# One softmax over three dilated groups, run between the quarters of its own projection

## The chip, the cores and the metric

The kernel runs on one core of a Trainium2 chip, in float32 from input to output. The metric is the device time of one execution, in microseconds (us). Engines: TensorE (PE in the profile, its weight loads PEld), VectorE (DVE), ScalarE (ACT), GpSimd (POOL) and SyncE (SP), which issues most DMAs.

## The reference, cut to what matters

512 positions of 1024 features go through two layers. Each layer is a mixer, a layer norm, a mixture of experts (top 2 of 32), and a layer norm. The change is in the second layer's mixer:

```
def odd_mixer(x, w_in, w_out):
    p = (x @ w_in).reshape(B, T, 3, 3, DIL_HEADS, DIL_DH)      # group, q/k/v, 8 heads of 64
    slopes = alibi_slopes(DIL_HEADS)
    for g, (window, dilation) in enumerate(((128,1), (512,4), (2048,16))):
        o, l = dilated_band_attention(p[:, :, g, 0], p[:, :, g, 1], p[:, :, g, 2],
                                      window, dilation, slopes)
        outs.append(o); lses.append(l)
    wts = jax.nn.softmax(jnp.stack(lses, 0), axis=0)
    y = jnp.einsum('gbth,gbthd->bthd', wts, jnp.stack(outs, 0))
    return y.reshape(B, T, DIL_W).astype(x.dtype) @ w_out
```

A query t of a group sees the keys t, t-d, t-2d, ... within the window, with scores q.k/8 minus slope times distance. Each group has its own softmax, and the three outputs are weighted by the softmax of their log-sum-exps. With 512 positions that is the same as one softmax over all keys of the three groups together.

## The kernel before, in words

x stands turned in `xt_hi` and `xt_lo`, the high and the low part of its numbers; each weight chunk is split likewise by ScalarE (`split_unit`, L676, the high part) and VectorE (L952, the rest), so that a product is three matmuls: hi x hi, hi x lo, lo x hi. A *unit* is half the contraction of 512 output features: four quarters of 12 matmuls of 128x512 each. The input projection of the second layer has 18 units (`chunk`, `unit`, matmuls on L1542), its results go to two alternating sets of four PSUM banks, and are copied out four at a time (`evacuate`, L682 and L960). SP loads a unit's weights (1 MB) when the split of the unit two before it has been done.

After the last unit attention begins. It goes over four pairs of heads, and for each pair over two heads and two layers of work (near: group 0, with 256 keys for each tile of 128 queries; far: groups 1 and 2, whose queries and keys are sorted by residue modulo 4, so that a tile holds one residue): 16 steps of four tiles. The queries of the other head of the pair are zero in `qz`, so that the contraction is 128. A step is: `odd_scores` (L1903 to L1910), `biased` (L1439, adds slope times distance and takes the maximum), `exps` (L906), `weights_t` (L1921, transposes), `keep_weights` (L916, L1450, PSUM to SBUF), `odd_mix` (L1935 to L1940), `keep_out` (L1457). Scores run one step ahead. Far and near have softmaxes of their own; the far rows are written to DRAM and read back in order of position, and the two are merged there by maxima and denominators (L1479 to L1500). Then y is turned (L1959), split in two parts and multiplied with the output weights (`out_and_logits`, L1648). Tile by tile VectorE adds the residual and takes the norm's statistics (`out_norm`, L1203 to L1212), ScalarE normalises, TensorE turns the rows (L1658) and computes the router's logits (L1666). The router's index arithmetic and the experts follow; SP loads the weights of the experts in three buffers, which overlap the tiles of the mixer, with `load_pair`.

Every engine has its list of instructions in program order; the order around the change is written out by hand, and semaphores tie the engines together.

## Time and profile before

| | us |
|---|---|
| median of 3 runs | 1295.38 (1289.61 to 1295.59) |
| the profiled execution | 1293.89, its span 1292.1 |
| TensorE matmul busy | 1050.3 (81%) |
| VectorE, ScalarE, POOL busy | 499.9, 296.4, 134.7 |
| mean granted TensorE clock | 0.916 of full speed |

Busy times of TensorE count overlapping matmuls once. Its matmuls are pipelined: a 128x512 matmul lasts 0.39 us and the next starts 0.23 us after it. The order of stages in time: first layer's mixer to about 285 us, its router and experts to 600, second layer's norm and projection to 820, attention and merge to 948, output projection, router, experts and the last norm.

### The profile page before, as it was taken

What the parts mean: (1) busy time and instruction counts of PE and PEld (TensorE: products, weight loads), DVE (VectorE), ACT (ScalarE), POOL (GpSimd) and SP (SyncE); (2) the same over time, 40 slices, a digit from 0 to 9 for tenths busy, and PEclk for the clock granted to TensorE, in tenths of its full rate; (3) what the DMA queues carried; (4) which work ended last, traced back from release to release, by engine and by line L of the source; (5) the groups of instructions that cost most, each with busy time, mean ns of one, the idle gap of its engine ahead of it and who ended that gap; (6) DMA issues with size and microseconds to landing.
All of it is one profiled execution on the core that took longest, in us unless ns stands there. A gap on an engine that the chain in (4) does not pass through costs nothing.

```text
span 1292.1 us, 14037 instructions
## 1 busy us (share of the span) xinstructions
PE 1050.3 (81%) x5044; PEld 717.8 (56%) x5044; DVE 499.9 (39%) x1201; ACT 296.4 (23%) x567; POOL 134.7 (10%) x191
## 2 busy tenths in 40 slices
PE   6999999998798788850999999688477788787850
PEld 5878888886343233320788889578466333233320
DVE  3853675555333111118422222454265333111118
ACT  3343312221112111110321212243211121111110
POOL 5000000000121111110000000121010111111110
PEclk8989999996899999995899999898677899999995
DMA  8244331449699999934233223000159699999943
GB/s 219 66 72 92 69 95 66 160 182 385 228 421 423 424 425 424 424 160 182 98 98 97 97 98 98 1 9 16 43 208 381 248 422 425 424 424 424 424 161 167
DMA packets 68845, 286.87 MB, mean 222 GB/s; under 512 B 12268, under 2 KB 14332, under 8 KB 43184
## 3 DMA queue, kind: packets, MB, share of 16 engines
q1 hardware_dynamic: 52992, 234.96, 48.2%
q10 hardware_dynamic: 5184, 33.56, 6.2%
q0 software_dynamic: 10608, 17.54, 3.7%
q8 instruction: 37, 0.61, 0.2%
q14 instruction: 24, 0.20, 0.0%
HBM read 281.79 MB, written 24.15 MB: 237 GB/s over the span
## 4 chain that ended last, share of the span: by engine, by line
PE 59%; DMA 14%; SPq 11%; DVE 9%; issue 5%; ACT 2%; ACTq 0%; POOLq 0%; DVEq 0%; POOL 0%
PE bank L1542 15%; PE bank L1621 14%; DMA wgu<-in_w_up 10%; PE bank L1822 8%; SPq L392 6%; SPq L397 4%; PE bank L1844 4%; PE bank L1648 4%; PE bank L1639 2%; DVE h L1380 2%; PE bank L1910 1%; PE bank L1723 1%; PE bank L1708 1%; PE bank L1811 1%; PE bank L1666 1%
## 5 line engine op out<-in xcount | busy, mean ns | idle before, releaser
L1822 PE MATMUL bank<-wgu,xgt 128*64 128x512 f32 x1024 | 234.3, 610 | 31.3 <-DMA wgu<-in_w_up 27.9
L1822 PEld LDWEIGHTS bank<-wgu,xgt 128*64 128x64 f32 x1024 | 86.1, 141 | 175.1 <-issue 159.3
L1844 PE MATMUL bank<-wd,htt 128*64 128x512 f32 x512 | 116.9, 597 | 49.9 <-issue 48.5
L952 DVE TENSOR_TENSOR wl<-raw,wh 128x2048 fp32r<-128x2048 f32 x40 | 91.6, 2290 | 146.4 <-ACT wh L676 146.4
L676 ACT ACTIVATE wh<-raw 128x2048 fp32r<-128x2048 f32 x40 | 76.6, 1915 | 192.5 <-PE bank L1621 104.8
L1346 DVE TENSOR_TENSOR hh<-sg,bank 128x256 f32<-128x256 f32 x32 | 13.5, 421 | 233.2 <-ACT sg L837 233.2
L1844 PEld LDWEIGHTS bank<-wd,htt 128*64 128x64 f32 x512 | 40.4, 136 | 104.3 <-issue 104.3
L1542 PE MATMUL bank<-xt_hi,wh 128*128 128x512 f32 x192 | 75.4, 393 | 2.7 <-DVE wl L952 2.7
L1542 PE MATMUL bank<-xt_hi,wl 128*128 128x512 f32 x192 | 75.2, 392 | 0.0
L1542 PE MATMUL bank<-xt_lo,wh 128*128 128x512 f32 x192 | 75.2, 392 | 0.0
L1351 DVE COPY yt<-bank 128x512 f32<-128x512 f32 x32 | 22.1, 692 | 135.1 <-PE bank L1844 135.1
L829 ACT ACTIVATE xgt<-bank,lnt 128x128 f32<-128x128 f32 x136 | 51.2, 456 | 70.3 <-PE bank L1811 70.3
L837 ACT ACTIVATE sg<-bank 128x256 f32<-128x256 f32 x32 | 12.3, 385 | 223.9 <-PE bank L1822 223.9
L1621 PE MATMUL bank<-xt_hi,wh 128*128 128x512 f32 x128 | 52.6, 411 | 7.4 <-DVE wl L952 7.4
L1338 DVE TENSOR_SCALAR xgt<-bank,lnt 128x128 f32<-128x128 f32 x136 | 46.4, 403 | 16.9 <-PE bank L1811 16.8
L1621 PE MATMUL bank<-xt_hi,wl 128*128 128x512 f32 x128 | 51.5, 402 | 0.0
L1621 PE MATMUL bank<-xt_lo,wh 128*128 128x512 f32 x128 | 51.3, 401 | 0.0
L1621 PE MATMUL bank<-wh,xt_hi 128*128 128x512 f32 x128 | 50.6, 395 | 0.0
L847 ACT ACTIVATE yt<-bank 128x512 f32<-128x512 f32 x32 | 19.1, 597 | 136.5 <-PE bank L1844 120.0
L1621 PE MATMUL bank<-wh,xt_lo 128*128 128x512 f32 x128 | 49.9, 390 | 0.0
L574 POOL DMA_INDIRECT y_rows<-yt,td x20 | 24.4, 1219 | 244.8 <-ACT yt L847 164.3
L1621 PE MATMUL bank<-wl,xt_hi 128*128 128x512 f32 x128 | 49.9, 389 | 0.0
(333 smaller groups left out, 1759.5 us busy)
## 6 DMA issues: line engine op xcount, KB each, us to landing
wgu<-in_w_gate SPq DMA_DIRECT2D x64, 1024.0 KB, 22.7
wgu<-in_w_up SPq DMA_DIRECT2D x64, 1024.0 KB, 25.7
wd<-in_w_down SPq DMA_DIRECT2D x36, 1024.0 KB, 25.4
wd<-in_w_down ACTq DMA_DIRECT2D x28, 1024.0 KB, 12.4
raw<-in_w_in_odd SPq DMA_DIRECT2D x18, 1024.0 KB, 4.9
raw<-in_w_in_even SPq DMA_DIRECT2D x16, 1024.0 KB, 7.3
y<-y_rows SPq DMA_DIRECT2D x8, 1024.0 KB, 8.5
h<-in_x SPq DMA_DIRECT2D x8, 512.0 KB, 5.1
```

The lines of the kernel that those rows point to most:

```text
L392: sp.dma_start(wgu[s][:, b, i, :, :].rearrange("p k f -> p (k f)"), w[l][ds(e, 1)].rearrange("a (p k) f -> p (a k f)", p=P)).then_inc(wgu_ ...
L397: sp.dma_start(wd[s][:, b, :, :].rearrange("p k n -> p (k n)"), w_down[l][ds(e, 1)].rearrange("a (p k) n -> p (a k n)", p=P)).then_inc(wd_ ...
L676: act.activation(wh[slot][:, :, :], raw[slot][:, :, :], ACT.Copy).then_inc(w_hi, 1)
L829: ins = act.activation(xgt[:, k, :], bank[0][:, k * P:(k + 1) * P], ACT.Identity, scale=lnt[:, l, 0, k:k + 1], bias=lnt[:, l, 1, k:k + 1])
L952: dve.tensor_tensor(wl[slot][:, :, :], raw[slot][:, :, :], wh[slot][:, :, :], ALU.subtract)\
L1338: ins = dve.tensor_scalar(xgt[:, k, :], bank[1][:, (k - 4) * P:(k - 3) * P], lnt[:, l, 0, k:k + 1], lnt[:, l, 1, k:k + 1], ALU.mult, ALU.add)
L1380: link(dve.scalar_tensor_tensor(h[:, t, :], y2[t][:, c * D:(c + 1) * D], ga[:, c, t:t + 1], h[:, t, :], ALU.mult, ALU.add))
L1542: ins = pe.matmul(out_of(i), a, b, start=(k == 0 and n == 0), stop=(k == nk - 1 and n == 2))
L1621: ins = pe.matmul(bank[i][:, :], a, b, start=(k == 0 and n == 0), stop=(k == 7 and n == 2))
L1648: ins = pe.matmul(bank[4 * c + t][:, :], yp[:, kk, t * P:(t + 1) * P], wp[c][:, kk, :], start=(first and kk == 0 and n == 0), stop=(kk == ...
L1822: ins = pe.matmul(bank[2][B * b:B * (b + 1), :], xgt[:, k, B * b:B * (b + 1)], wgu[s][:, b, :, k, :], start=(k == 0), stop=(k == KT - 1))
L1844: ins = pe.matmul(bank[5 + n][B * b:B * (b + 1), :], htt[:, k, B * b:B * (b + 1)], wd[s][:, b, k, n * 512:(n + 1) * 512], start=(k == 0), ...
```

## The change

All eight heads get one softmax over the 512 columns that a tile of 128 queries has: 256 near keys, 128 of group 1 and 128 of group 2. The step is now one tile of a pair of heads (`n` from 0 to 15: pair `n // 4`, tile `n % 4`), both heads at once, each in its own half of the array's rows (64 features), with no zero padding. In each tile the queries stand by residue modulo 4 (32 of each), so that a far product is 32 queries of one residue by the 128 keys of that residue, written to 32 of the bank's partitions. Slopes move into the queries' scale and the exponential's scale, so that one table of distances serves all heads. The weights are turned by a product with a diagonal that holds 1 over the denominator. The mix gives the heads' outputs already turned (64 features by 512 positions, two heads one above the other), so that the merge, the far rows in DRAM and the turning of y are gone.

The projection goes in another order: q and k of the first four heads of the three groups, then v for the far groups and for group 0, then q and k of the other four heads and the rest of v. All its chunks use banks 0 to 3, emptied tile by tile (`keep_odd`), and banks 4 to 7 hold the scores. Attention's steps stand between quarters of units 6 to 17 (`q(m, i)`), by an order written out for each engine. The output projection starts with the first features while the last pair is being done. SP loads the first experts' gate and up weights before the output projection; one pair of experts, not two, is loaded behind it.

```diff
+        ODD = ((0, 0), (1, 0), (2, 0), (None, 0), (None, None), (0, 1), (1, 1), (2, 1), (None, 1))
@@ SyncE
+            for m in range(18):
+                (g, o), u = ODD[m // 2], U_ODD + m
+                sp.wait_ge(w_lo, u + 1)
+                w = xo[m % 2 * 4 * P:(m % 2 + 1) * 4 * P, :]
+                if o is None:
+                    src = w[:, 2 * C:3 * C].rearrange("(k p) c -> p k c", p=P)
+                    sp.dma_start(raw[m % 2][:, :, :], src).then_inc(raw_in[m % 2], 16)
+                    continue
+                src = w.rearrange("(k p) (g s o c) -> p k g s o c", p=P, g=3, s=3, o=2)
                 for i in range(2):
-                    for half in range(2):
-                        load_unit(4 * g + (U_ODD + 2 * i + half), half, xo, half * 4 * P,
-                                  ds(g * (3 * C) + i * C, C))
-            for g in range(3):
-                for half in range(2):
-                    load_unit(U_ODDV + 2 * g + half, half, xo, half * 4 * P,
-                              slice(3 * C * g + 2 * C, 3 * C * (g + 1)))
+                    part = src[:, :, i + 1, 2, o, :] if g is None else src[:, :, g, i, o, :]
+                    sp.dma_start(raw[m % 2][:, :, 256 * i:256 * (i + 1)], part).then_inc(raw_in[m % 2], 16)
...
+            sp.wait_ge(unit_done, U_WOUT2 + 2)
+            load_gate_up(1, 0, (0, 1))
+            sp.wait_ge(w_lo, U_WOUT2 + 2 + 2)
+            load_down(1, 0, (0, 1))
+            sp.wait_ge(yl, 4)
             load_pair(1, 2, (4, 5))
             sp.wait_ge(unit_done, U_WOUT2 + 2 + 2)
-            load_pair(1, 0, (0, 1))
             load_pair(1, 1, (2, 3))
...
@@ POOL
+            for t in (2, 3):
+                wait_ln(pool, 1, t)
+            pool.iota(near0[:, :], pattern=[[1, 256]], base=-P, channel_multiplier=-4, **exact)
+            for i in range(2):
+                pool.iota(near1[:, i, :], pattern=[[4, 224]], base=-4 * 96, channel_multiplier=-4, **exact)
+            pool.iota(jdiff[:, :], pattern=[[-1, 224]], base=224, channel_multiplier=1).then_inc(near_ready, 1)
...
@@ ScalarE
+            def keep_odd(c, i):
+                if i < 3:
+                    act.wait_ge(bank_done, 3 * (8 + c) + i + 1)
+                else:
+                    act.wait_ge(unit_done, U_ODD + 2 * c + 4)
+                g, o = ODD[c]
+                if o is None:
+                    ins = act.activation(v3[:, 0, i, :], bank[i][:, :], ACT.Copy)
+                elif g is None:
+                    ins = act.activation(v3[:, 1:3, i, 256 * o:256 * (o + 1)],
+                                         bank[i][:, :].rearrange("p (g c) -> p g c", g=2), ACT.Copy)
+                elif g == 0:
+                    ins = act.activation(kg0[:, 2 * o + i - 2, :], bank[i][:, :], ACT.Copy)
+                else:
+                    ins = act.activation(k12[:, 2 * o + i - 2, g - 1, :].rearrange("p (a j) -> p a j", a=4),
+                                         perm(bank[i][:, :]), ACT.Copy)
+                ins.then_inc(kept[i], 1)
+            def exps(n):
+                hp, t = divmod(n, NT)
+                act.wait_ge(nm_ready, n + 1)
+                for b in range(2):
+                    s = sc[n % 2][b][:, (0 if t else P):T]
+                    ins = act.activation(s, s, ACT.Exp, scale=SLOPES[2 * hp + b], bias=nm[:, n, b:b + 1],
+                                         accum_out=dn[:, n, b:b + 1])
...
+            def keep_weights(n):
...
+                act.activation(pts[hp // 3][0][:, T * t + lo:T * (t + 1)], bank[4 + 2 * (n % 2)][:, lo:T], ACT.Copy)\
+                   .then_inc(pta, 1)
+            def heads_hi(hp):
+                act.wait_ge(o2_ready, hp + 1)
+                act.activation(in_row_order(yo_hi[:, hp, :]), in_step_order(bank[3 if hp == 2 else 6][:, :]), ACT.Copy).then_inc(yh, 1)
...
+            for m in range(16):
+                if m:
+                    split_unit(U_ODD + m + 1, (m + 1) % 2)
+                if 6 <= m < 14:
+                    exps(m - 6)
+                if m in (10, 14):
+                    heads_hi((m - 10) // 4)
+                if m % 2:
+                    keep_odd(m // 2, 2)
+                if 6 <= m < 14:
+                    keep_weights(m - 6)
+                if m % 2:
+                    keep_odd(m // 2, 3)
+            split_unit(U_ODD + 17, 1)
+            exps(8)
+            exps(9)
+            keep_weights(8)
+            exps(10)
+            keep_weights(9)
+            exps(11)
+            keep_weights(10)
+            split_unit(U_WOUT2, 0)
+            exps(12)
+            keep_weights(11)
+            exps(13)
+            keep_weights(12)
+            exps(14)
+            keep_weights(13)
+            keep_odd(8, 2)
+            keep_odd(8, 3)
+            exps(15)
+            keep_weights(14)
+            heads_hi(2)
+            split_unit(U_WOUT2 + 1, 1)
+            keep_weights(15)
+            heads_hi(3)
...
@@ VectorE
+            def q_scales():
+                for i in range(8):
...
+                dve.wait_ge(near_ready, 1)
+                far_ = near_t[:, :].rearrange("p (g c) -> p g c", g=2)
...
+            def biased(n):
...
+                for b in range(2):
+                    s, d = bank[4 + 2 * (n % 2) + b], sc[n % 2][b]
+                    dve.tensor_tensor_reduce(out=d[:, lo:256], in0=s[:, lo:256], in1=near0[:, lo:256],
+                                             scale=1.0, scalar=-3.0e38, op0=ALU.add, op1=ALU.max,
+                                             accum_out=mm[:, n, b, 0:1])
+                    ins = dve.tensor_tensor_reduce(out=d[:, 256:T].rearrange("p (g c) -> p g c", g=2),
+                                                   in0=s[:, 256:T].rearrange("p (g c) -> p g c", g=2),
+                                                   in1=near1[:, :, 96 - 32 * t:224 - 32 * t],
                                                    scale=1.0, scalar=-3.0e38, op0=ALU.add, op1=ALU.max,
-                                                   accum_out=mm[lay][:, t:t + 1])
+                                                   accum_out=mm[:, n, b, 1:2])
+            def diagonals(n):
+                dve.wait_ge(p_ready, n + 1)
+                link(dve.reciprocal(rd[:, n, :], dn[:, n, :]))
+                for b in range(2):
+                    ins = dve.tensor_scalar(dg[n % 2][b][:, :], ident[:, :], rd[:, n, b:b + 1], None, ALU.mult)
+                ins.then_inc(dg_ready, 1)
...
+            def heads_lo(hp):
+                dve.wait_ge(yh, hp + 1)
+                dve.tensor_tensor(in_row_order(yo_lo[:, hp, :]), in_step_order(bank[3 if hp == 2 else 6][:, :]),
+                                  in_row_order(yo_hi[:, hp, :]), ALU.subtract).then_inc(yl, 1)
+            for m in range(16):
+                if m:
+                    split_unit(U_ODD + m + 1, (m + 1) % 2)
+                if m == 1:
+                    q_scales()
+                if m == 2:
+                    distances()
+                if m % 2:
+                    keep_odd(m // 2, 0)
+                if 6 <= m < 14:
+                    biased(m - 6)
+                if m % 2:
+                    keep_odd(m // 2, 1)
+                if 6 <= m < 14:
+                    diagonals(m - 6)
+                if m in (10, 14):
+                    heads_lo((m - 10) // 4)
+                if 6 <= m < 14:
+                    keep_weights(m - 6)
...
+            biased(12)
+            keep_weights(11)
+            diagonals(12)
+            keep_odd(8, 0)
+            biased(13)
+            keep_weights(12)
+            diagonals(13)
+            keep_odd(8, 1)
+            biased(14)
+            keep_weights(13)
+            diagonals(14)
+            biased(15)
+            keep_weights(14)
+            diagonals(15)
+            heads_lo(2)
+            split_unit(U_WOUT2 + 1, 1)
+            keep_weights(15)
+            heads_lo(3)
...
@@ TensorE
+            def odd_part(v, tiles):
+                c, half, slot = v // 2, v % 2, v % 2
+                g, o = ODD[c]
...
+                for i in tiles:
+                    if half == 0 and c:
+                        pe.wait_ge(kept[i], 8 + c)
+                    for kk in range(4):
+                        k = 4 * half + kk
+                        for n, (xp, wp) in enumerate(((xt_hi, wh), (xt_hi, wl), (xt_lo, wh))):
+                            if o is None:
+                                a, b = in_order(xp, k, i), wp[slot][:, kk, :]
+                            elif g is None:
+                                a, b = by_residue(xp, k, i), wp[slot][:, kk, :]
+                            else:
+                                a, b = wp[slot][:, kk, i * P:(i + 1) * P], xp[:, k, :]
+                            ins = pe.matmul(bank[i][:, :], a, b, start=(k == 0 and n == 0), stop=(k == 7 and n == 2))
+                    if half and i < 3:
+                        ins.then_inc(bank_done, 1)
+                if tiles[-1] == 3:
+                    ins.then_inc(unit_done, 1)
+            def odd_scores(n):
+                hp, t = divmod(n, NT)
+                st = 4 + 2 * (n % 2)
+                if t == 0:
+                    for i in (hp % 2, 2 + hp % 2):
+                        pe.wait_ge(kept[i], 8 + (8 if hp > 1 else 3))
+                if n >= 2:
+                    pe.wait_ge(pta, n - 1)
+                    pe.wait_ge(ptd, n - 1)
...
+                rows_of = [slice(64 * b, 64 * (b + 1)) for b in range(2)]
+                for b, r in enumerate(rows_of):
+                    lo = 0 if t else P
+                    pe.matmul(bank[st + b][:, lo:256], qg0[r, hp, t * P:(t + 1) * P],
+                              kg0[r, hp, (t - 1) * P + lo:(t + 1) * P], start=True, stop=True)
+                for g in range(2):
+                    for a in range(4):
+                        for b, r in enumerate(rows_of):
+                            ins = pe.matmul(bank[st + b][32 * a:32 * (a + 1), 256 + g * P:256 + (g + 1) * P],
+                                            q12[r, hp, g, t * P + 32 * a:t * P + 32 * (a + 1)],
+                                            k12[r, hp, g, a * P:(a + 1) * P], start=True, stop=True)
...
+            def weights_t(n):
+                t, st = n % NT, 4 + 2 * (n % 2)
+                pe.wait_ge(dg_ready, n + 1)
+                for k in range(0 if t else 1, 4):
+                    for b in range(2):
+                        ins = pe.matmul(bank[st + b][:, k * P:(k + 1) * P], sc[n % 2][b][:, k * P:(k + 1) * P],
+                                        dg[n % 2][b][:, :], start=True, stop=True)
...
+            def odd_mix(hp):
...
+                out_of = [bank[3 if hp == 2 else 6][64 * b:64 * (b + 1), :] for b in range(2)]
+                cols = [slice((2 * hp + b) * DH, (2 * hp + b + 1) * DH) for b in range(2)]
+                for s in (0, 2, 1, 3):
+                    w = 1 if s == 3 else 2
+                    for b in range(2):
+                        at = T * s + P
+                        src = pts[hp // 3][b][:, at:at + P] if s == 3 else \
+                            pts[hp // 3][b][:, at:at + 2 * 384].rearrange("p (u c) -> p u c", u=2)[:, :, 0:P]
+                        pe.matmul(out_of[b][:, s * P:(s + w) * P], v3[:, 0, s, cols[b]], src,
+                                  start=(s == 0), stop=False)
+                for g in range(2):
+                    for a in range(4):
+                        for b in range(2):
+                            at = 256 + g * P + 32 * a
+                            ins = pe.matmul(out_of[b].rearrange("p (t c) -> p t c", t=NT)[:, :, 32 * a:32 * (a + 1)],
+                                            v3[:, 1 + g, a, cols[b]],
+                                            pts[hp // 3][b][:, :].rearrange("p (t c) -> p t c", t=NT)[:, :, at:at + 32],
+                                            start=False, stop=(g == 1 and a == 3))
...
+            def odd_out(t, c, kks):
+                for kk in kks:
+                    for n, (yp, wp) in enumerate(((yo_hi, wh), (yo_hi, wl), (yo_lo, wh))):
+                        ins = pe.matmul(bank[4 * c + t][:, :], yp[:, kk, t * P:(t + 1) * P], wp[c][:, kk, :],
+                                        start=(kk == 0 and n == 0), stop=(kk == 3 and n == 2))
+                return ins
+            for m in range(16):
+                n = m - 6
+                q(m, 0)
+                if 0 <= n < 8:
+                    odd_scores(n)
+                q(m, 1)
+                if m in (10, 14):
+                    odd_mix((m - 10) // 4)
+                q(m, 2)
+                if 0 <= n < 8:
+                    weights_t(n)
+                q(m, 3)
+            q(16, 0)
+            odd_scores(8)
+            q(16, 1)
+            odd_scores(9)
+            weights_t(8)
...
+            odd_scores(14)
+            weights_t(13)
+            q(17, 3)
+            odd_scores(15)
+            weights_t(14)
+            odd_mix(2)
+            def first_features(t):
+                pe.wait_ge(kept[t], 17)
+                odd_out(t, 0, range(2))
+            pe.wait_ge(w_lo, U_WOUT2 + 3)
+            first_features(0)
+            first_features(1)
+            weights_t(15)
+            first_features(2)
+            odd_mix(3)
+            pe.wait_ge(yl, 3)
+            first_features(3)
+            pe.wait_ge(w_lo, U_WOUT2 + 4)
+            odd_out(0, 1, range(3))
+            odd_out(0, 0, (2,))
+            pe.wait_ge(yl, 4)
+            for t in range(NT):
+                odd_out(t, 1, range(0 if t else 3, 4))
+                last = odd_out(t, 0, range(2 if t else 3, 4))
+                if t < 3:
+                    last.then_inc(tile_out, 1)
+                else:
+                    last.then_inc(unit_done, 2)
+            normed_logits(1)
```

## Rows read from the trace of the kernel before

**Rows 1.** The page: TensorE's busy share, the granted clock in 40 slices.

```profile
PE 1050.3 (81%) x5044; PEld 717.8 (56%) x5044; DVE 499.9 (39%) x1201; ACT 296.4 (23%) x567; POOL 134.7 (10%) x191
...
PEclk8989999996899999995899999898677899999995
```

**Rows 2.** Chain of waits, second mixer: start, length, work (xcount: instructions).

```profile
620.75 199.10 PE bank L1542 x864
...
851.54 0.88 PE bank L1921 x8
852.42 1.79 PE bank L1910 x16
...
947.62 23.81 PE bank L1648 x96
```

**Rows 3.** Stretches: length; busy PE, PEld, DVE, ACT, POOL; clock; DMA.

```profile
819.90:830.20 10.30, 0.00 (x0) 0.00 (x0) 7.84 (x6) 4.14 (x4) 0.00 (x0) 0.75 0.00 0
830.20:923.60 93.40, 78.74 (x552) 74.07 (x552) 43.60 (x191) 39.33 (x144) 18.59 (x15) 0.88 0.03 9
923.60:942.50 18.90, 0.11 (x2) 0.00 (x0) 8.71 (x16) 0.46 (x2) 5.79 (x4) 0.51 0.27 73
942.50:947.60 5.10, 3.68 (x16) 3.28 (x16) 4.55 (x7) 3.13 (x5) 0.00 (x0) 0.50 0.43 146
```

**Rows 4.** Groups by shape, 818 to 935 us: busy us, mean ns, idle before.

```profile
L906 ACT ACTIVATE sc<-sc,nm 128x256 f32<-128x256 f32 x56 | 27.7, 495 | 30.9 <-DVE nm L1443 30.9
L1439 DVE CUSTOM_DVE_ANT_0 sc<-bank,bh 128x256 f32<-128x256 f32 x56 | 20.5, 420 | 8.0 <-PE bank L1910 7.3 <-issue 0.7
...
L906 ACT ACTIVATE sc<-sc,nm 128x128 f32<-128x128 f32 x8 | 3.2, 397 | 16.6 <-DVE nm L1443 16.6
```

**Rows 5.** Chain of waits: first projection, tiny matmuls; expert products, transposes behind.

```profile
48.78 16.33 PE bank L1621 x72
...
78.04 1.02 PE bank L1600 x32
...
1015.51 7.09 PE bank L1822 x32
...
1029.26 6.87 PE bank L1822 x32
1036.12 1.09 PE bank L1811 x8
```

**Rows 6.** Groups by shape of VectorE and ScalarE, 620 to 822 us.

```profile
L952 DVE TENSOR_TENSOR wl<-raw,wh 128x2048 fp32r<-128x2048 f32 x19 | 43.5, 2291 | 85.9 <-ACT wh L676 85.9
...
L959 DVE TENSOR_SCALAR q<-bank 128x512 f32 x4 | 2.6, 686 | 13.5 <-PE bank L1542 13.5
...
L676 ACT ACTIVATE wh<-raw 128x2048 fp32r<-128x2048 f32 x19 | 36.4, 1918 | 76.1 <-PE bank L1542 76.1
```

**Rows 7.** The page's DMA issues: count, KB each, us to landing.

```profile
raw<-in_w_in_odd SPq DMA_DIRECT2D x18, 1024.0 KB, 4.9
```

**Rows 8.** Timeline of SP: first expert weights behind the output projection.

```profile
971.46 0.33 SPq L392 DMA_DIRECT2D wgu<-in_w_gate  x1
```

**Rows 9.** DMA rate from 900 to 1040 us in 40 slices.

```profile
GB/s 7 68 5 0 0 0 0 84 166 143 0 2 19 360 426 424 424 150 0 180 176 338 394 425 427 421 438 421 433 419 335 276 25 67 0 222 428 419 406 423
```

**Rows 10.** Timeline of VectorE: the last output tile's statistics, first and last.

```profile
971.47 1.29 DVE L1203 SCALAR_TENSOR_TENSOR h<-h,bank 128x512 f32<-128x512 f32 x2 [0.28 <-PE bank L1648]
...
976.48 0.16 DVE L1212 SCALAR_TENSOR_TENSOR nmr<-mv,rstd 128x1 f32<-128x1 f32 x1
```

**Rows 11.** Stretches of the first layer, columns as in rows 3.

```profile
68.00:70.00 2.00, 2.00 (x4) 0.35 (x2) 1.93 (x3) 0.00 (x0) 0.00 (x0) 0.50 1.02 158
70.00:72.00 2.00, 2.00 (x6) 1.61 (x6) 1.48 (x3) 1.08 (x2) 0.44 (x1) 0.50 0.83 128
...
140.00:160.00 20.00, 20.00 (x99) 16.50 (x98) 16.27 (x51) 8.00 (x18) 2.79 (x1) 1.00 0.30 53
```

**Rows 12.** Timeline of TensorE, first layer: products with 4 rows.

```profile
65.05 5.01 PE L1586 MATMUL bank<-mrow,sel 4*128 4x512 f32 x8
```

More of the change, by code:

```diff
@@ L125, in trunk @@
         mask = const.take("mask", [P, P], f32)
-        near = const.take("near", [P, 2, 256], f32)
+        near0 = const.take("near0", [P, 256], f32)
         before = const.take("before", [P, P], bf16)
@@ L145, in trunk @@
         eq = lngb_z.take("eq", [P, 8, NCOL], f32)
+        lngb_z = Zone(const.at, 8 * KB)
+        sc = [[lngb_z.take(f"sc{i}{b}", [P, T], f32) for b in range(2)] for i in range(2)]
         lngb_z = Zone(const.at, 8 * KB)
@@ L1461, in pair_steps @@
-            def pair_steps(hp, last):
-                for k in range(4):
-                    if not (last and k == 3):
-                        biased(hp, k + 1)
-                    keep_weights(hp, k)
-                    if k:
-                        keep_out(hp, k - 1)
-                keep_out(hp, 3)
-            biased(0, 0)
-            with dve.Fori(0, 3) as hp, link.rolled(hp, 4, 3):
-                pair_steps(hp, False)
-            pair_steps(3, True)
-            dve.wait_ge(far_in, 32)
@@ new lines, in _ @@
+            split_unit(U_ODD + 17, 1)
+            biased(8)
+            diagonals(8)
+            biased(9)
+            keep_weights(8)
+            diagonals(9)
+            biased(10)
+            keep_weights(9)
+            diagonals(10)
+            biased(11)
+            keep_weights(10)
+            diagonals(11)
+            split_unit(U_WOUT2, 0)
+            biased(12)
[4 more added lines that the diff above has]
+            keep_weights(12)
@@ L1550, in by_residue @@
                 return perm(xp[:, k, :])[:, i, :]
-            def chunk(c, a, u, st, x_cols=None, xt_from=None):
-                pe.wait_ge(ev_d, c + 1)
-                if a is not None:
-                    pe.wait_ge(ev_a, a + 1)
-                for half in range(2):
-                    unit(u + half, half, half, lambda i: bank[st + i][:, :], x_cols, xt_from=xt_from)
             pe.wait_ge(ident_ready, 1)
```

442 lines of the change are left out of this document (121 added, 321 removed).

## The prediction

> **What bounds the kernel now.** I read the row of busy shares and the granted clock in forty slices first [rows 1]: TensorE is busy 81% of the span, and the stretch of slices 26 to 30 is where it is idle or slow. The chain of waits over the second layer's mixer then gives the stage [rows 2]. The projection is one piece of TensorE work, 199.10 us from 620.75, with nothing between its 864 matmuls. The output projection starts at 947.62 and takes 23.81 us, so it ends at 971.43. The 127.8 us between (947.62 - 819.85) are attention alone. The table of stretches splits them [rows 3]: 10.3 us with TensorE idle while the padded queries are staged; 93.4 us of head steps with TensorE busy 78.7 us at a mean clock of 0.88; 18.9 us in which it works 0.11 us (far rows to DRAM and back, merge); and 5.1 us of turning y at clock 0.50. The whole mixer, 620.75 to 971.43, takes 350.7 us. Behind it stand the router and then the experts, whose weights stream at 424 GB/s.
>
> So attention pays latencies in turn: scores, biasing, exponentials, weights turned, copied, mixed. The change puts these steps between quarter units of the projection. What counts then is TensorE's own work, if every latency fits behind it.
>
> **TensorE's work after the change.**
> - Projection: again 18 units of 48 matmuls, and again 192 of them read x by residue. 199.1 us stays.
> - Near scores: 32 products with a contraction of 64 rows, two heads on the two halves of the array. Full-array products of this type cost 1.79 us for 8 with 128 columns (16 instructions), 0.224 each [rows 2], so 0.448 for 256 columns. In turn: 24 x 0.448 + 8 x 0.224 = 12.5 us; side by side 6.3 (the first tile of each pair has 128 near keys).
> - Far scores: the tile's queries stand by residue, so each residue has a product of 32 queries by 128 keys: 16 per tile for two heads and two groups, 256 in all. At the full-array price 256 x 0.224 = 57.3 us. No row shows 64*32 pieces of the array. The nearest is the expert product in two 64-column halves: 16 products of 512 columns take 6.87 us, 0.429 each [rows 5], where 512 columns at 0.224 per 128 would be 0.896; two halves run as one. The lower bound is issue: 32 tiny matmuls take 1.02 us, 0.032 each [rows 5], and each product is two instructions, so 512 x 0.032 = 16.4 us. I take factor two, the nearest row: 28.7 us for far, 6.3 for near, 35.0 together; bounds 22.7 (6.3 + 16.4) and 69.8.
> - Weights turned: no longer transposes (0.88 us for 8) but products with a diagonal of 1/denominator, 1.79 us for 8 [rows 2]: (16 x 8 - 4 x 2) x 0.224 = 26.9 us, where transposes would cost 13.2. This edit costs time, and buys the whole merge.
> - Mixing: output 64 rows high, two heads in the two column halves, the case that [rows 5] shows. Near 24 x 0.448 + 8 x 0.224 = 12.5, far 64 x 0.224 = 14.3; halved, 13.4 us.
> - Output projection: 96 matmuls, now without a cold start. 72 in 16.33 us is 0.2268 each [rows 5]: 21.8 us.
> - Changes of the array's shape: three per tile and two per mix, 16 x 3 + 4 x 2 = 56. After the expert product in halves, 8 transposes take 1.09 us, in the attention loop the same 8 take 0.88 [rows 2, 5]: 0.21 for a return to the full shape, of which there are 20. The 36 others have no row; bounds nothing and 0.21, I take half. Together 4.2 + 3.8 = 8.0 us.
>
> Sum: 199.1 + 35.0 + 26.9 + 13.4 + 21.8 + 8.0 = 304.2 us against 350.7: 46.5 us less.
>
> The Trainium skill (TensorEngine Tiling, Key Properties) says that changing the tiling mode drains the engine, which speaks against this change; the 0.21 us agrees in kind, and without any such cost the forecast would be 8 us lower. The same skill (TensorE: Matmul & The Clock Gate, part 3) has 16 pieces of 32 by 32 run 10.6 times as fast; by it the far scores would fall to their lower bound, and the time would be that of the first rival below. No row here shows it or excludes it.
>
> **Does every latency fit?** One unit is 48 x 0.2268 = 10.9 us, a quarter 2.72. In units 6 to 13 a step is quarter, scores (2.2), quarter, quarter, weights, quarter. From the end of scores to the weights there are two quarters, 5.4 us. In that time VectorE does four reductions (56 in 20.5 us, 0.37 each [rows 4]: 1.5) and two small operations (0.3), ScalarE two exponentials of 512 (256 take 0.50, 128 take 0.40 [rows 4], so 0.69 each, and 0.2 for reading the sum: 1.6), VectorE the reciprocal and two diagonals (0.6, an estimate: three operations near the 0.2 us that its small ones take), handovers 0.4: 4.4 us. VectorE is free to start: the split of the next unit ends about 1.9 + 2.3 us after the unit begins, plus 0.7 for a kept bank [rows 6], near 5.0, when scores end too (2.72 + 2.2). Slack some 1 us. Of VectorE's 15 us step, at most 2.3 + 1.8 + 0.6 + 0.7 + 1.4 = 6.8 are used. All projection chunks now share four banks; each is emptied by 0.69 us three quarters before it is needed.
> In units 16 and 17 a tile's period is 2.72 + 2.2 + 1.8 + 0.45 = 7.2 us on TensorE; VectorE, in order, needs its 4.4 us loop per tile plus 2.3 twice for splits. It fits. Past the last quarter, the last tile's latency stands behind its scores, turned weights, mix 2 and two pieces of the output projection, about 8 us; mix 3 waits for a weight split and two copies, and here I see the two sides within 0.5 us. I allow 2 us for such waits over the whole mixer.
>
> **Moved or added, hidden.** SP's queue: the weights come in half loads with 1 KB runs, two issues a unit; a unit's load took 4.9 us in the page's DMA list [rows 7] and has the rest of one unit and a whole one, about 17 us, so it may double. Four stores to the far rows, two small ones and two loads go. The first pair of experts is now issued before the output projection and only one pair remains after it; before, the two pairs issued from 971.46 kept DMA near its full rate to about 1005, dropping to 25 GB/s by 1010, and the experts began at 1015.5 [rows 5, 8, 9], so this gains nothing and loses nothing. POOL stages nothing; its five tables are written right after the norm and read two units later. VectorE's sixteen memsets and thirteen distance operations (about 5 us) stand in units 1 and 2, which have over 5 us free each. In the first layer POOL and VectorE lose some set-up; there the chain is TensorE without a gap, so 0.
>
> **Late behind it.** Output tiles now end 12.2, 8.1, 4.1 and 0 us before the end (18 matmuls each) rather than in pairs. VectorE needs 5.2 us from a tile to its statistics [rows 10]. Tile 1 ends its at -2.9 (two rows of sums 2.9, scale 2.3), tile 2 at +2.3, tile 3 at +7.5 where it was +5.2 (971.47 to 976.64). The last normalised tile is turned at once if late; before it had 4.5 us to spare, but tile 2 delays the turning too. I charge 2.2 us.
>
> Gain 46.5 - 2 - 2.2 = 42.3 us. The profiled run took 1293.89 us (span 1292.1), 1.5 under the median of 1295.38, within the spread of the three runs. That gives 1251.6 on the profiled run and 1253 on the median: I forecast 1252.
>
> **Rivals.**
> 1. The small pieces run eight at a time. Scores cost 22.7, not 35.0: 12.3 less, 1240. For: independent halves already run fully beside each other [rows 5]. Against: two heads write different banks from the same columns, which no row shows. Then VectorE's 4.4 us loop is still under the 6.4 us period.
> 2. They run in turn. Scores cost 69.8: 34.8 more, 1287. For: only column halves are shown, never rows split. Against: the halves in [rows 5].
> 3. Slower than before, by the clock. Around 67 us TensorE was busy all the time with products of 4 rows and the clock still fell to 0.50 (68 to 72 us) [rows 11, 12]: being busy does not hold it. Score stretches of 2 us with 64 by 32 pieces recur for over 190 us. Each us of full-speed work done at 1.2 GHz costs one more, so from 42.3 us of such work on (a fifth of the interleaved stretch of some 200 us) the change loses; at a half of it, 100 us, it is 1252 + 100 = 1352. Against: in the first layer attention between projection quarters ran at 1.00 throughout (140 to 160 us) [rows 11], and here every gap is filled with full-array work.
> 4. It does not overlap as it says: some step's latency is over 5.4 us, and TensorE waits at each of 16 tiles. At 1.5 us each, 24 us: 1276. Against: the slack worked out.
>
> **Chances.** Forecast 0.52, rival 1 0.20, rival 2 0.11, rival 3 0.06, rival 4 0.11. Rivals 1, 2 and 4 all stay faster; of rival 2 and 4 together a little would come to no change. Under 0.5% (6.5 us, what the runs can tell) I put 0.05, slower 0.06, faster 0.89. Range 1235 to 1283: it holds rivals 1 and 4 and leaves out rival 3 and most of rival 2.
>
> **What would show it.** Near and far scores of a tile: 2.2 us if factor two, 1.4 if eight, 4.4 in turn. Projection matmuls 0.227 apart at clock 1.00 throughout. TensorE busy without gaps from 621 to about 927, and the output projection ending there instead of at 971. Everything behind it shifted and equally long. A mean clock under 0.9 in that stretch, or VectorE as releaser of the diagonal products in many tiles, would prove me wrong.

## Result, and the profile after

The changed kernel took 1232.08 us (median of 4 runs, 1228.44 to 1235.47) against 1294.35 for the kernel before: ratio 0.9514, interval 0.949 to 0.9537. The forecast was 1252 with a range of 1235 to 1283: the sign was right, the gain 20 us too small, and the time 3 us below the range. The profiled execution took 1234.14 us, 59.8 less than the 1293.89 before.

The page of the changed kernel, busy time of each engine, then TensorE and its granted clock in forty slices, answers to [rows 1]:

```profile
PE 1033.2 (84%) x5484; PEld 690.9 (56%) x5484; DVE 493.3 (40%) x1237; ACT 288.8 (23%) x501; POOL 107.4 (9%) x159
...
PE   6999999999688878875199999999996888787850
...
PEclk8989999998699999998599999999986999899985
```

Slices 21 to 30 hold the mixer: TensorE full and at full clock, where before slices 26 to 30 were partly idle or slow. The stretches below answer to [rows 3]; columns are busy us and instructions of PE, PEld, DVE, ACT and POOL, the granted clock, DMA share and GB/s.

```profile
620.50:690.10 69.60, 69.60 (x300) 57.85 (x300) 25.59 (x46) 16.34 (x14) 0.00 (x0) 0.98 0.33 106
690.10:832.30 142.20, 142.20 (x987) 118.95 (x986) 54.79 (x135) 43.13 (x63) 0.00 (x0) 1.00 0.23 75
832.30:883.00 50.70, 49.95 (x541) 43.06 (x541) 30.03 (x117) 20.18 (x44) 0.00 (x0) 1.00 0.24 89
883.00:907.10 24.10, 24.10 (x147) 19.93 (x146) 13.09 (x30) 4.87 (x6) 0.00 (x0) 1.00 0.95 367
907.10:955.50 48.40, 35.18 (x153) 25.98 (x151) 25.25 (x123) 8.23 (x16) 6.77 (x7) 0.68 0.57 218
955.50:1232.40 276.90, 196.42 (x928) 83.98 (x928) 76.44 (x143) 45.35 (x113) 35.82 (x45) 0.91 0.84 350
```

The whole mixer now takes 286.6 us (620.5 to 907.1) in place of 350.7, which is 64.1 less; from the output projection's end to the first expert product it is 48.4 in place of 44.1, 4.3 more; the experts take 276.9, before 276.6 (1292.1 - 1015.5). 64.1 - 4.3 = 59.8: that is the whole difference.

The chain of waits in the first interleaved steps (start, us, what) answers to the first line of [rows 2]:

```profile
620.49 69.73 PE bank L1863 x300
690.22 0.42 PE bank L1883 x4
690.64 0.60 PE bank L1888 x32
691.24 5.96 PE bank L1863 x24
697.20 1.34 PE bank L1898 x12
...
718.97 0.63 PE bank L1883 x4
719.61 0.60 PE bank L1888 x32
720.20 5.67 PE bank L1863 x24
725.87 1.78 PE bank L1898 x16
727.65 5.47 PE bank L1863 x24
```

L1883 is the near scores, L1888 the far ones, L1863 the projection, L1898 the turned weights. In these steps nothing but TensorE is in the chain. The far scores of a tile, 16 products in 32 instructions, take 0.60 us; I had put them at 1.8 (28.7 over 16 tiles).

Matmuls overlap, so the busy time of a group overstates what it costs; where the text below says *start to start*, it counts from the start of a matmul to the start of the next. The groups over the whole mixer (line, engine, names, piece of the array, shapes, count | busy, mean ns | idle before):

```profile
L1898 PE MATMUL bank<-dg,sc 128*128 128x128 f32 x240 | 30.1, 278 | 0.1
...
L1888 PE MATMUL bank<-k,q 64*32 64x128 f32 x512 | 10.7, 275 | 0.0
L1883 PE MATMUL bank<-kg,qg 64*128 64x256 f32 x48 | 8.4, 428 | 0.6 <-ACT pts L865 0.6
```

### The profile page after: what moved, and what is told of

It reads as the page before. It is cut to its first block, busy times and chain, and to the rows that moved or that the text cites. A ratio compares the mean times of both kernels' runs of the same rounds, so it can differ in the third digit from the quotient of the medians.

```text
span 1232.4 us, 14337 instructions
## 1 busy us (share of the span) xinstructions
PE 1033.2 (84%) x5484; PEld 690.9 (56%) x5484; DVE 493.3 (40%) x1237; ACT 288.8 (23%) x501; POOL 107.4 (9%) x159
## 4 chain that ended last, share of the span: by engine, by line
PE 61%; DMA 14%; SPq 11%; DVE 9%; issue 4%; ACT 2%; POOLq 0%; ACTq 0%; POOL 0%; DVEq 0%
PE bank L1863 16%; PE bank L1579 15%; DMA wgu<-in_w_up 11%; PE bank L1783 9%; SPq L409 6%; SPq L414 4%; PE bank L1805 4%; PE bank L1898 2%; PE bank L1597 2%; PE bank L1606 2%; DVE h L1338 2%; PE bank L1684 1%; PE bank L1669 1%; PE bank L1624 1%; PE bank L1772 1%
## 5 line engine op out<-in xcount | busy, mean ns | idle before, releaser
L1863 PE MATMUL bank<-xt_hi,wh 128*128 128x512 f32 x192 | 76.5, 399 | 2.6 <-DVE wl L925 2.6
L1863 PE MATMUL bank<-xt_lo,wh 128*128 128x512 f32 x192 | 75.3, 392 | 0.0
L1863 PE MATMUL bank<-xt_hi,wl 128*128 128x512 f32 x192 | 75.2, 392 | 0.0
L792 ACT ACTIVATE sg<-bank 128x256 f32<-128x256 f32 x32 | 12.3, 383 | 223.5 <-PE bank L1783 223.5
L1296 DVE TENSOR_SCALAR xgt<-bank,lnt 128x128 f32<-128x128 f32 x136 | 46.4, 403 | 15.9 <-PE bank L1772 15.7
L802 ACT ACTIVATE yt<-bank 128x512 f32<-128x512 f32 x32 | 19.1, 597 | 137.5 <-PE bank L1805 106.0
L1772 PEld LDWEIGHTS bank<-ident,xg 128*128 128x128 f32 x272 | 32.9, 194 | 29.1 <-issue 26.0
```

The source lines that it names most:

```text
L1296: ins = dve.tensor_scalar(xgt[:, k, :], bank[1][:, (k - 4) * P:(k - 3) * P], lnt[:, l, 0, k:k + 1], lnt[:, l, 1, k:k + 1], ALU.mult, ALU.add)
L1772: ins = pe.transpose(bank[k // 4][:, (k % 4) * P:(k % 4 + 1) * P], xg[s][:, k:D:KT], ident[:, :])
L1863: ins = pe.matmul(bank[i][:, :], a, b, start=(k == 0 and n == 0), stop=(k == 7 and n == 2))
```

## Experiments

Each is the changed kernel with one edit. "Mixer" is the stretch from the first projection matmul to the end of the output projection in the profiled execution, 286.6 us in the changed kernel; "behind" is from there to the first expert product, 48.4.

**The far scores twice.**

```
-                for g in range(2):
+                for g in (0, 1, 0, 1):
                     for a in range(4):
                         for b, r in enumerate(rows_of):   # far product of group g, column piece a, head b
```

> The changed kernel with the 16 far products of each of the 16 tiles computed twice, everything else the same. Theory A (the 64 by 32 pieces run eight at a time, a tile's far scores cost TensorE 0.60 us): 16 x 0.60 = 9.6 us more, 1241 to 1243 on 1232. Theory B (they run at factor two, and 0.60 us is only how the records show it, the rest being spread over the matmuls that follow): 512 instructions at 0.056, 28.7 us more, about 1261. Theory C (the scores lie beside other work, TensorE is not what sets the stage): no change, 1232. Between the ends A and C lies what the last tiles' latencies hide.

Measured: 1240.05 us, ratio 0.9562 [0.953, 0.9593], against 0.9514 about 6 us more, with both intervals 3 to 4 us wide to either side. Each tile's far scores take 1.09 in place of 0.60 (as in the first row of the next experiment): the second pass costs 0.49, 7.8 us over 16 tiles. The groups of matmuls behind them take what they took before (5.67 and 5.47 us around the turned weights), so the short time is not a debt paid later; the mixer of the profiled execution is 292.4 us, 5.8 more, although the changed kernel's had 2.9 us at half clock near its start and this one had none. Theory A, and a little under it; B and C fall.

**Which pieces run beside each other.** A row half is the 64 rows of one head, a column piece 32 partitions of the output; together they are eight pieces. The cut is abridged: it gives the kind of repetition that tile `n` gets.

```
+                again = {0: the 16 products in the kernel's order, 1: [(i % 2, 0, 0) for i in range(16)],
+                         2: [(i // 2 % 2, 0, i % 2) ...], 3: [(i // 4 % 2, i % 4, 0) ...], ...}[n % 8]
+                for g, a, b in again:
+                    ins = far(g, a, b)
```

> The changed kernel; each tile computes some of its scores once more, in a different order for tiles n = 0 to 7 of each eight: 16 far products again (0) in the kernel's order, (1) all on one 64 by 32 piece, (2) on the two row halves of one column piece, (3) on the four column pieces of one row half, (4) order column piece, group, row half, (5) order row half, group, column piece, (6) order column piece, row half, group; (7) four near products of 256 columns per head again. Read from the trace of each tile. If pieces are what gives the speed: in turn on one piece 32 instructions at about 0.11 = 3.5 us, two pieces 1.8, four 0.9, eight 0.45 to 0.6; orders 4 and 6 cost more than 0.6 if TensorE starts instructions strictly in order (each piece's next product waits for its last: 5 to 9 slots of 0.11 to 0.15 us in place of 4), and 0.6 if it does not. If pieces are not what counts (an instruction of 32 columns is simply short), all of (0) to (6) cost the same. Near: 4 x 0.42 / 2 for each pair, about 0.42 to 0.45 us per pair of 256 columns in place of the 0.32 between pairs. Total time about 20 us over the changed kernel, 1245 to 1260.

Measured: 1255.94 us, one run. The chain's rows of the eight kinds, in the order of n = 0 to 7 (the far scores and their repetition are one piece of 64 instructions; in tile 7 the near product stands by itself in L1899):

```profile
690.19 1.08 PE bank L1888 x64
...
704.98 4.04 PE bank L1888 x64
...
723.10 2.30 PE bank L1888 x64
...
738.95 1.46 PE bank L1888 x64
...
753.75 1.27 PE bank L1888 x58
...
771.77 1.24 PE bank L1888 x59
...
786.56 1.29 PE bank L1888 x58
...
801.42 0.60 PE bank L1888 x32
802.02 1.93 PE bank L1899 x16
```

Less the 0.60 of the regular pass, 32 instructions cost 3.44 us on one piece (0.108 each, about what an instruction of 128 columns costs on the full array, 1.79 / 16 in [rows 2]), 1.70 on two row halves, 0.86 on four column pieces and 0.48 on all eight: 2.0, 4.0 and 7.2 times as fast. Rows split as well as columns do. The other orders of the same 16 products on all eight pieces cost 0.67, 0.64 and 0.69, and tiles 8 to 15 repeat every one of these values. In the order of tile 6, four instructions in a row belong to one piece; starts strictly in that order would take 8 x 3 x 0.108 = 2.6 us. So other pieces do go ahead; whether TensorE's queue or the compiled order does that, the trace does not tell. The Trainium skill (TensorE: Matmul & The Clock Gate, Part 3, The mechanism) has matmuls start and end strictly in order; the 0.69 does not bear that out for this program. Near products run two heads side by side at 1.93 / 4 = 0.48 for 256 columns each.

**Transposes in place of products with a diagonal.** VectorE scales the weights, TensorE only turns them (a line that sets `lo` is left out).

```
-                    ins = dve.tensor_scalar(dg[n % 2][b][:, :], ident[:, :], rd[:, n, b:b + 1], None, ALU.mult)
+                    w = sc[n % 2][b][:, lo:T]
+                    ins = dve.tensor_scalar(w, w, rd[:, n, b:b + 1], None, ALU.mult)
-                        ins = pe.matmul(bank..., sc[n % 2][b][:, k * P:(k + 1) * P], dg[n % 2][b][:, :], ...)
+                        ins = pe.transpose(bank..., sc[n % 2][b][:, k * P:(k + 1) * P], ident[:, :])
```

> The changed kernel with the weights normalised by VectorE (two multiplications of 512 columns in place of the two diagonals) and then turned by transposes in place of products with a diagonal. TensorE: 120 blocks at 0.11 in place of 0.21, 13 us less. VectorE's loop between scores and turning grows by 2 x (0.35 to 0.69 - 0.2), 0.3 to 1.0 us, to about 5; the cover is 5.4 in the interleaved steps and 4.4 among the last eight tiles. Theory A (TensorE's own work sets the stage, covers hold): the eight interleaved tiles give 6.6 us, the last eight give some part of 6.6: 1219 to 1226. Theory B (the latency loop sets the pace already, above all among the last eight tiles): no gain or a loss, 1230 to 1240.

Measured: 1224.18 us, ratio 0.9444 [0.9413, 0.9475]; mixer 276.1, 10.5 less. The group of 240 instructions above is now this one:

```profile
L1900 PE MATMUL bank<-ident,sc 128*128 128x128 f32 x120 | 16.2, 277 | 0.4 <-DVE sc L1424 0.4
```

TensorE's turning fell from 26.4 to 12.5 us start to start, 13.9 less; 10.5 of it came through. Theory A, with 3.4 us kept, most of it by waits in the last eight tiles. The longest is 2.2: one quarter of the projection took 5.35 us before the next scores began, in place of 3.8 in the changed kernel and 3.1 without a wait. These scores wait for ScalarE's copy of turned weights, which stands behind the next tile's exponentials; those wait for VectorE's reductions, which stand behind the split of the output weights.

**Logits of tiles 0 and 1 before tile 2 is turned** (second layer's router only; ScalarE's order changed to match).

```
-                    for t in range(3): turn_normed(l, t)
-                    for t in range(3): logits(l, t)
+                    turn_normed(l, 0); turn_normed(l, 1); logits(l, 0)
+                    turn_normed(l, 2); logits(l, 1); logits(l, 2)
                 turn_normed(l, 3)
```

> The changed kernel with, in the second layer's router alone, another order on ScalarE (normalise 0, 1, keep turned 0, 1, then tile 2) and TensorE (turn 0, 1, logits 0, turn 2, logits 1, 2, turn 3, logits 3). Theory A (what the late output tiles cost is that the logits of tiles 0 to 2 wait for tile 2's statistics and then run at a clock of 0.50): logits start at +2 us after the output projection in place of +5.2, and the stretch to the first expert product shrinks from 48.4 to 42 to 45 us: 1226 to 1229. Theory B (only tile 3's statistics count, 7.4 us after the output projection): its turning then follows at +9 in place of +16.6, but tile 2's logits stand behind; the same 3 to 6 us less. Theory C (DMA sets when the experts start, by the second pair of weights): no change, 1232.

Measured: 1225.05 us, ratio 0.9464 [0.9433, 0.9496]; behind 39.0 in place of 48.4. The cause in A and B is the same queue of logits, and both gave 3 to 6; it was 9.4 in the profiled execution, where the clock stood higher too (0.86 in place of 0.68, rows below), and 7.0 in the medians. How much of the 9.4 is the order and how much the clock was not separated; against the 44.9 of two kernels with the old order and a clock of 0.77 it is 5.9. The experts started when the router let them: C falls.

**The latency loop made 1.4 us longer.** The four biased reductions of a tile are done twice.

```
+                for b in range(2):  # the same two tensor_tensor_reduce once more, to the same places
+                link(ins)
                 for b in range(2):
```

> The changed kernel with VectorE's four biased reductions of a tile done twice, one after the other: 1.5 us more between a tile's scores and its diagonals, no work more for TensorE. It prices the cover of the latency loop. Theory A (the loop is 4.4 us and the cover 5.4 in the interleaved steps, 4.4 to 5 among the last eight tiles): 0.5 us more at each of eight tiles and 1 to 1.5 at the last eight, 12 to 16 us: 1244 to 1248. Theory B (much slack is left, the loop is nearer 3 us): under 4 us, 1232 to 1236. Theory C (no slack, TensorE already waits at each tile): 1.5 x 16 = 24 us, 1256.

Measured: 1246.73 us, ratio 0.9612 [0.9576, 0.9648]; mixer 302.0, 15.4 more. Theory A. TensorE's waits, without the one at the mixer's start, are now

```profile
PE bank L1909 <- DVE dg L1433: 6.1, 7, 1.4
PE bank L1894 <- ACT pts L865: 5.1, 5, 2.4
```

11.2 us at 12 places, where the changed kernel has 0.6 at one. Part of the rest is the clock: it stood at 0.50 from 871.0 to 877.8, which the changed kernel does not show and which costs up to 3.4. The chain of that kernel in an interleaved step shows what starts the loop:

```profile
700.00 1.93 ACT wh L638
...
701.95 2.29 DVE wl L925
704.24 0.60 DVE v L1389
704.84 0.33 DVE sc L1404
...
708.12 1.53 ACT sc L855 x4
...
709.67 0.17 DVE rd L1431
...
709.88 0.49 DVE dg L1433 x2
...
710.41 2.05 PE bank L1909 x16
```

VectorE comes to a tile's scores only after the split of the next weights and a kept bank (704.84, scores done at 703.9). The changed kernel's own trace gives the slack directly. In the same tile its diagonals are done at 710.44:

```profile
709.96 0.48 DVE L1422 TENSOR_SCALAR dg<-ident,rd 128x128 f32<-128x128 f32 x2
```

TensorE starts on them at 711.33, 0.9 us later. Over the 16 tiles this slack is 0.4 to 1.3 us in seven of the eight interleaved ones (4.6 in the one with a mix in between), 0.06 in tile 8, 1.1 to 1.9 in tiles 9 to 14 and 4.0 in the last. I had "some 1 us".

**The attention behind the projection instead of inside it**, same instructions, two tiles in flight. Of the order only TensorE's part is shown; ScalarE's and VectorE's were changed to match.

```
+            for m in range(18):
+                for i in range(4): q(m, i)
+            for n in range(16):
+                odd_scores(n)
+                if n: weights_t(n - 1)
+                if n in (4, 8, 12): odd_mix(n // 4 - 1)
```

> The changed kernel with all of the second layer's attention behind the projection in place of inside it; instructions and buffers are the same, two tiles are in flight. Theory A (both the new arithmetic and the overlap count): TensorE still has 87 us less to wait for than its 127.8 us of attention before, but each tile now has only the next tile's scores (1.2 us) and the turning of the one before (1.7) to hide VectorE's and ScalarE's loop of about 4.4 us. Two tiles in flight with scores 1.2 + loop 4.4 + turning 1.7 + copy 0.7 = 8.0 us make 4.0 a tile against 2.95 of TensorE's work: 16 x 1.05 = 17 us longer than the changed kernel, 1249; VectorE with 3.1 us of work a tile and its handovers may make it 4.5 a tile, 1257. Theory B (the gain is the overlap alone; the same arithmetic in turn is no better than before): 1285 to 1300. Theory C (the overlap is worth nothing, two tiles in flight hide all): 1232.

Measured: 1272.06 us, ratio 0.9822 [0.9776, 0.9868]; mixer 324.7. None of the three: a tile took 5.2 to 5.8 us, not 4.0 to 4.5. The next scores wait for the copy of the weights turned before, and on ScalarE that copy stood behind exponentials that themselves wait for VectorE (53.5 us in all by the list of waits). So the kernel was run again with the copy first:

```
+                if n: keep_weights(n - 1)
                 exps(n)
-                if n: keep_weights(n - 1)
```

> The kernel with the attention behind the projection, and on ScalarE each tile's copy of the turned weights ahead of the next tile's exponentials instead of behind them. In the earlier order a tile took 5.3 to 5.5 us: the next scores wait for the copy of the weights turned last, and that stood behind exponentials which themselves wait 2 us for VectorE. Theory A (the queue order on ScalarE alone made it 5.5; the loop is 4.4 us with two tiles in flight): 4.0 to 4.3 us a tile, 16 x 1.2 = 19 us less, 1250 to 1256. Theory B (VectorE's and ScalarE's own sum sets the tile): about 5 us a tile, 1262 to 1268. Theory C (no change): 1272.

Measured: 1263.43 us, ratio 0.974 [0.9714, 0.9767]; mixer 316.0. Its chain over one tile:

```profile
851.69 2.07 PE bank L1847 x16
853.76 0.02 issue
853.78 0.60 ACT pts L865
854.38 1.41 ACT sc L855 x4
855.79 0.02 issue
855.81 0.18 DVE rd L1399
855.99 0.02 issue
856.01 0.49 DVE dg L1401 x2
856.51 0.04 issue
856.55 2.07 PE bank L1847 x16
```

Tile to tile 4.86 us: turned weights, their copy, the next exponentials, reciprocal, diagonals. The copy first lets go the scores but holds the exponentials, so either order on ScalarE closes a loop through TensorE, ScalarE and VectorE. My theory A missed that loop; B's figure is right and its reason (sums of work) is not. Between these kernels the new arithmetic is worth 350.7 - 316.0 = 34.7 us without the overlap (the clock is in it: its mean was 0.92 in the mixer of the kernel before and 0.98 here), and the overlap 316.0 - 286.6 = 29.4 more.

**The changed kernel once more.**

> The changed kernel itself once more, on the same chip as the others: 1228 to 1236. It is there for the stretch between the output projection and the first expert product, which was 48.4 us in the changed kernel's profile but 44.8 with the far products doubled and 44.9 with transposes, where the clock stayed at 0.50 for 13.7 us in place of 20.5 behind the output projection. Theory A (the difference is the clock's alone, and differs between executions of one kernel): 44.8 or 48.4 again, with 13.7 or 20.5 us of 0.50. Theory B (it belongs to this kernel): 48.4 and 20.5 us.

Measured: 1233.62 us, ratio 0.9508 [0.947, 0.9547]; behind 48.2, with 20.5 us at clock 0.50 again: B. The stretches behind the output projection, of this execution, of the far scores twice, of the logits early, and of the kernel before, in that order:

```profile
906.20:954.40 48.20, 33.76 (x153) 25.30 (x152) 25.24 (x123) 8.26 (x16) 6.80 (x7) 0.71 0.55 219
```
```profile
907.50:952.40 44.90, 30.99 (x155) 22.33 (x154) 25.25 (x123) 8.34 (x16) 6.86 (x7) 0.77 0.60 234
```
```profile
901.80:940.80 39.00, 26.23 (x155) 18.37 (x153) 25.23 (x123) 8.28 (x16) 6.83 (x7) 0.86 0.69 263
```
```profile
971.30:1015.50 44.20, 31.52 (x153) 22.91 (x152) 23.30 (x110) 7.90 (x15) 6.81 (x7) 0.73 0.89 349
```

Same work, and TensorE busy 2.8 us longer where the clock (third from the right) is 0.71 and not 0.77. The changed kernel had the slower stretch in both of its profiled executions; why the doubled far scores, and the transposes (44.9 us at 0.77 too), move it, no run settled.

**Both gains in one kernel**, transposes and the early logits, the latter in both layers.

> The changed kernel with both of the earlier edits, weights scaled by VectorE and turned by transposes (7.9 us less alone) and the logits' new order (7.0 less alone), the latter now in both layers' routers. If the edits add up and the first layer's router gains nothing: 1217. If the first layer's router gains as the second's did, its turning of the last tile no longer behind three logits: 1211 to 1214. If the gains overlap (both shift the same wait): 1221 to 1224.

Measured: 1217.53 us (4 runs, 1212.03 to 1225.42), ratio 0.9398 [0.9341, 0.9455]: the fastest of all, 1.2% under the changed kernel. Mixer 275.9, behind 41.7: 10.7 and 6.7 less, where the two edits alone gave 10.5 and 9.4. In the medians the gains add up, but the interval is 7 us wide to either side and excludes none of the three cases. The first layer's router does gain in the profile: from its output projection to the first expert product it is 41.0 us, 44.2 in the changed kernel and 43.4 to 44.8 in all the others:

```profile
292.60:333.60 41.00, 26.57 (x154) 18.55 (x152) 23.30 (x110) 7.87 (x15) 6.77 (x7) 0.84 0.94 378
```

That 3.2 does not reach the time of this execution, in which the second layer's experts took 280.0 in place of 276.9; why they did stays open.

## Why the prediction was wrong

The failed step is one term of TensorE's sum, "I take factor two, the nearest row: 28.7 us for far". Start to start in the changed kernel's trace:

- Far scores 9.8 us, not 28.7: the pieces run eight at a time, 7.2 times as fast as in turn. The Trainium skill (TensorE: Matmul & The Clock Gate, Part 3, Measured speedup vs the span model) gives 10.6 for sixteen; the trace agrees in kind, and I had let it decide nothing. The measured 9.8 is also below the 16.4 us that I gave as a lower bound from issue at 0.032 each: 512 instructions at 0.019, 0.015 in the second pass. That row was of tiny matmuls of another form; it bounded their own spacing, not the issue of others. This is rival 1, which I had at 0.20 and 12.3 us for all scores; they came to 19.1 in place of 35.0, 15.9 less, and the far ones alone 18.9 less. With 9.8 in place of 16.4, rival 1 would have stood at 1233 and not 1240, and a range ending at 1235 could not have held it.
- Near scores 9.3, not 6.3: 0.48 for 256 columns of both heads in place of 0.45, and some 0.15 a tile for the change of shape, which I had counted elsewhere.
- Projection 205.4 in all, 6.3 over 199.1: the two groups of 24 around the turned weights take 5.67 + 5.47 in the chain where 48 at 0.2267 are 10.88, 0.26 a tile; in the last two units each quarter of 12 takes 3.1 in place of 2.82; one waits another 0.7. If all of that but the wait is put to changes of shape, they come to some 8 us with the 0.15 of the near scores; I had 8.0. Another 0.11 a tile lies inside the 9.8 of the far scores.
- Weights turned 26.4 (26.9 expected), mixing 13.7 (13.4), output projection 22.2 (21.8).
- "2 us for such waits": 0.6 by the group above, which is the wait in the one quarter just named; it is already in the terms. The loop of 4.4 us was right where VectorE is free: from the end of a tile's scores to its diagonals 4.2 us in six of the last eight tiles. In the interleaved steps it is 4.5 to 5.1, since VectorE comes late, which leaves less than the "some 1 us" in most. Rival 4 was near: another 1.4 us of loop cost 15, a part of it by the clock.
- "Late behind it: I charge 2.2": 4.2 in this kernel. Statistics end 7.4 us after the output projection, as worked out (7.5). What I did not price is that tile 3's turning then waits behind three tiles of logits at half clock.

Together: far 18.9 less, near 3.0 more, the rest 3.6 less, 19.5 for the mixer; 2.0 more behind it. 1251.6 - 17.5 = 1234.1, the profiled execution.

Rival 3 (the clock falls) did not come: 1.00 from 690 to 907, though short products recur every 15 us. With the attention behind the projection (first order), where TensorE waits some 2 us at each tile, it did fall, for 24 us in all; the stretch of its 16 tiles:

```profile
817.20:921.40 104.20, 74.59 (x980) 60.11 (x979) 51.94 (x228) 36.66 (x86) 0.00 (x0) 0.89 0.11 42
```

With the copy first the same stretch, and there the clock was at 0.50 for 10.2 us:

```profile
817.20:911.20 94.00, 68.86 (x976) 55.05 (x976) 49.92 (x227) 36.25 (x86) 0.00 (x0) 0.95 0.12 46
```

So of the 29.4 us that the overlap is worth at most some 5 are the clock.

## What to carry to other kernels

Where a term rests on how far pieces of the array run beside each other and the profile before has no such row, both ends must stay in the range, and a "lower bound" from another shape's spacing is no bound. Products that fit in a part of the array's rows and columns cost little on TensorE once all pieces are used in turn: here a seventh of their time on one piece. An attention whose steps take turns on three engines gains from being cut into the gaps of independent work, but measure the slack of the loop (by making one engine's part longer): here it was 0.4 to 1.3 us in most interleaved steps, and a loop 1.4 us longer was paid at 12 places. A queue's order that looks free (copy or exponentials first) can close a loop through three engines.

## What the runs showed of the hardware

- 64 by 32 pieces: 32 instructions of 128 columns take 3.44 us on one piece, 1.70 on two, 0.86 on four, 0.48 on eight; records of eight pieces start 7 ns apart. Instructions of one piece in a row do not hold up those of others: 0.64 to 0.69 in three other orders.
- A change of shape costs 0.1 to 0.2 us: far scores 0.60 the first time and 0.49 the second, a pair of near products 0.63 behind the projection and 0.48 behind other near products. The Trainium skill (TensorEngine Tiling, Key Properties) says that a change of the mode drains TensorE; these are the prices.
- A transpose of 128 by 128 (one instruction) takes half of a product with a diagonal (two): 0.104 against 0.22 us, start to start.
- The clock behind the output projection stays at 0.50 for 20.5 us in the changed kernel, twice, and 13.7 in two variants that differ only ahead of it. By half of the difference, that is 3.4 us with no other difference in the work; the stretches differ by 3.3 to 3.5.
